# Moving half of an output projection's split weights and passes into the end of a gated scan, and the inverse root of two norms from logarithm and exponential

## The chip, the core and the metric

One core of one Trainium2 chip runs the whole program as one launch. The metric is the device time in microseconds of that launch. Five engines work side by side, each through its own list of instructions in order: TensorE (PE: matrix products, with its weight loads as PEld), VectorE (DVE), ScalarE (ACT), GpSimd (POOL) and SyncE (SP, which here only starts transfers). They wait for one another by semaphores.

## The reference, cut to what matters

The program is a deep stack; the change touches one stage of its second block and the norm ahead of two stages. For a stream of 256 tokens and a context of 256 tokens, with width 1024, that stage computes

```python
h = rms_norm(x, w) * (1 + scale) + shift            # y = x * rsqrt(mean(x*x) + 1e-6) * w
a = attention(h)                                    # 8 heads of 64: 512 columns
b = gated_scan(h)                                   # 4 heads of 128: 512 columns
x = x + gate * rms_norm(concat([a, b]) @ w_out, w2) # w_out: 1024 x 1024
```

Each head of the scan goes over all 512 tokens in two directions. A state decays by a factor per key column and token and takes in key times value; a query reads it. The kernel computes this as products between tokens with decays between them. A head's result is divided by its root mean square over its 128 columns and multiplied with a gate. The second block ends in a feed-forward part, and a second stage (local attention) follows with the same kind of norm ahead of it.

## The kernel before, in words

**Phases.** The program is a row of phases (`phase`, L200). Each has one instruction list per engine, and a barrier of all engines stands between two phases. Semaphores are the phase's own.

**Precision.** Products that need more than one pass are made from split numbers: `hi` is the value rounded to fp32r by a ScalarE copy, `lo` the rest, by a VectorE subtraction, and a product is hi x hi + hi x lo + lo x hi, three passes.

**The scan, `hgrn_phase` (L2782).** Four heads (`BH`), and for each eight units `u`: four tiles of 128 tokens in each of two directions. `sums` (L2945) makes the sums of the decays' logarithms in banks 0 to 2 of PSUM, `decay_tile` (L3106) is the ScalarE exponential that takes them, `products` (L3254) are the four VectorE products with keys and queries, `scores` (L2958) the TensorE products within sub-tiles (in bank 3, with the larger fragments in banks 4 and 5), `probs` (L3272) the VectorE mask and sum, `place` (L3209) the POOL product that puts them into the tile, `score_ends` (L3114) ScalarE's copies of the larger fragments, and `values` (L2983) the TensorE product with the values, added up in bank 7 (`O`). TensorE's list runs them with lags written out by hand: in unit u `sums(u)`, `scores(u-1)`, `values(u-3)`; between them, where a next head exists (`more`), the projection of that head (`slot`, L2914), a piece a unit. In the last head there is none.

**The end of a head (L3033 to L3048).** What one tile gives another is one set of six products per direction: `cross_operands` (L3282, VectorE), `cross_scores` (L2994, six products of fp32, which are twelve passes, into `X_PS`, bank 4 on), `keep_cross` (L3124, ScalarE, into `px`), `cross_values` (L3002, twelve passes into bank 7). Then `norm` on ScalarE (L3128: four squares with their sums, and a root) and VectorE (L3292), `turn_out` (L3009, four transposes) and `keep_output` (L3136), which writes the head's 128 columns into `y_T`. Chunks 0 to 3 of `y_T` are the attention's, and are there when the scan begins; chunks 4 to 7 are the four heads. SP loads the first four 512 KB blocks of `w_out` into `raw` (the space of `h_T`) at the end of its list (`load_ahead`, L2908).

**The projection, `out_both_phase` (L3338).** For each chunk n of 128 rows ScalarE makes `y_hi` and `w_hi` (L3389, L3391) and VectorE `y_lo` and `w_lo` (L3399, L3400). TensorE then has, for stream 0, twelve passes of 512 columns a chunk (two tiles of tokens, two halves of the columns, three parts) in banks 0 to 3; then the same for stream 1 in banks 4 to 7: 192 passes in all. After chunk 2 of stream 1 (`BEHIND`) it turns stream 0's scaled result (`turn_tensor`, L294). The last four blocks of `w_out` are asked for as their slots come free. The scalings behind are `post_scalar` (L328) and `post_vector` (L361).

**The pre-norm, `prenorm_phase` (L1994),** is called for the scan's stage (`first`) and for the second stage (with `bias`: there TensorE also makes a bias table, `Bias.products` L1971, which ScalarE and VectorE copy out, `Bias.keep` L1982). ScalarE squares five of eight tiles (L2027), VectorE three, and adds; TensorE sums over the partitions (L2058, L2060); ScalarE takes the root (L2031), VectorE the reciprocal (L2082), then h = x * r (L2088) and scale and shift on both engines (L2042, L2093). TensorE fills its idle time with products of zeros (`idle_products`, L305): 13, and 4 where there is a bias.

## Time and profile before

| | us |
|---|---|
| median of 3 runs | 2385.87 (2382.46 to 2386.08) |
| the profiled execution | 2385.46 |
| its span, first to last instruction | 2383.7 |
| PE busy | 2283.5 (96%) |
| DVE busy | 1442.6 (61%) |
| ACT busy | 1137.2 (48%) |
| POOL busy | 81.3 (3%) |
| mean granted clock of TensorE | 0.979 |

All times of one instruction are from the profiled execution and count from the start of its span. PE is busy 96% of the span as a whole, so what an edit is worth shows only in the stretch where it acts. The granted clock is a share of 2.4 GHz: 1.00 is 2.4 and 0.50 is 1.2 GHz. A matrix product of plain fp32 shows as two passes. Passes overlap: the time between two starts, not the length of one, is what a pass costs in a row of them. "L" and a number is a line of the kernel.

### The profile page before, as it was taken

The page shows a single profiled execution, that of the slowest core. Times are in us where ns is not written, and L with a number is a line of the kernel's source. Part 1 is how long each engine was busy: PE and PEld are TensorE (multiplying, and loading weights), DVE is VectorE, ACT ScalarE, POOL GpSimd, SP SyncE. Part 2 cuts the span into 40 slices and gives each one's busy share as a digit, 9 for nine tenths or more (in the row PEclk, how much of TensorE's full clock was granted, in tenths as well). Part 3 has the DMA queues.
Part 4 walks back from the last instruction along what each step waited for, and adds up shares of the span by engine and source line. Part 5 has one row for each costly group of instructions (what it writes and reads, how often), then busy time and mean ns, then how long its engine had stood idle before and what let it go on. Part 6 is the DMA issues. An engine that isn't in the chain of part 4 may idle for free. (4 is left out here: it accounts for less than half of the span.)

```text
span 2383.7 us, 37825 instructions
## 1 busy us (share of the span) xinstructions
PE 2283.5 (96%) x14434; PEld 1861.4 (78%) x14434; DVE 1442.6 (61%) x2358; ACT 1137.2 (48%) x1957; POOL 81.3 (3%) x117
## 2 busy tenths in 40 slices
PE   8999999999999999999999996999999989989998
...
GB/s 268 272 261 204 115 54 247 266 227 179 261 250 206 109 124 212 255 254 86 52 34 46 46 55 36 54 124 124 114 107 113 146 85 89 98 11 158 194 193 89
DMA packets 389939, 346.84 MB, mean 146 GB/s; under 512 B 24388, under 2 KB 353464, under 8 KB 389304
## 3 DMA queue, kind: packets, MB, share of 16 engines
...
HBM read 344.05 MB, written 1.05 MB: 145 GB/s over the span
## 5 line engine op out<-in xcount | busy, mean ns | idle before, releaser
L716 PE MATMUL ps<-x_hi_lo,gu_hi 128*128 128x512 f32 x1680 | 423.7, 394 | 3.3 <-DVE gu_sum L914 3.3
L716 PEld LDWEIGHTS ps<-x_hi_lo,gu_hi 128*128 128x128 f32 x1680 | 305.7, 188 | 82.4 <-issue 19.3
L914 DVE TENSOR_REDUCE gu_sum<-ps 128x256 f32<-128x512 f32 x220 | 150.1, 689 | 241.0 <-PE ps L718 240.8
L817 ACT ACTIVATE gu_hi<-w_gu 128x1024 fp32r<-128x1024 f32 x220 | 229.2, 1054 | 119.0 <-DMA w_gu<-in_ffn_w_up 45.1
L897 DVE TENSOR_TENSOR gu_lo<-w_gu,gu_hi 128x1024 fp32r<-128x1024 f32 x220 | 260.8, 1219 | 18.0 <-ACT gu_hi L817 17.7
L718 PEld LDWEIGHTS ps<-x_hi_lo,gu_lo 128*128 128x128 f32 x1680 | 228.8, 190 | 16.8
L718 PE MATMUL ps<-x_hi_lo,gu_lo 128*128 128x256 f32 x1680 | 233.8, 282 | 0.0
L745 PE MATMUL ps<-dn_hi,h_hi 128*128 128x512 f32 x440 | 173.3, 394 | 2.4 <-DVE h_lo L941 2.4
L745 PE MATMUL ps<-dn_lo,h_hi 128*128 128x512 f32 x440 | 172.5, 392 | 0.0
L745 PE MATMUL ps<-dn_hi,h_lo 128*128 128x512 f32 x440 | 171.3, 389 | 0.0
L833 ACT ACTIVATE silu<-gu_sum 128x256 f32<-128x256 f32 x88 | 36.7, 417 | 258.9 <-DVE gu_sum L914 258.3
L905 DVE TENSOR_TENSOR dn_lo<-w_dn,dn_hi 128x1024 fp32r<-128x1024 f32 x110 | 134.4, 1222 | 15.4 <-ACT dn_hi L821 10.7
L821 ACT ACTIVATE dn_hi<-w_dn 128x1024 fp32r<-128x1024 f32 x110 | 115.6, 1055 | 55.1 <-PE ps L745 55.1
L1077 PE MATMUL ps<-both_x_hi,gu_lo 128*128 128x512 f32 x320 | 124.5, 389 | 0.0
L1077 PE MATMUL ps<-both_x_lo,gu_hi 128*128 128x512 f32 x320 | 124.5, 389 | 0.0
L1077 PE MATMUL ps<-both_x_hi,gu_hi 128*128 128x512 f32 x320 | 124.5, 389 | 0.0
L1244 DVE SCALAR_TENSOR_TENSOR conv<-ps,par,conv 128x510 f32<-128x510 f32 x44 | 30.9, 744 | 129.4 <-ACT conv L1184 129.4
L745 PEld LDWEIGHTS ps<-dn_hi,h_hi 128*128 128x128 f32 x440 | 83.0, 189 | 17.9 <-issue 3.5
L745 PEld LDWEIGHTS ps<-dn_hi,h_lo 128*128 128x128 f32 x440 | 82.7, 188 | 18.1
L1184 ACT ACTIVATE conv<-ps,par 128x512 f32<-128x512 f32 x44 | 31.8, 775 | 131.7 <-PE ps L1077 121.0
L745 PEld LDWEIGHTS ps<-dn_lo,h_hi 128*128 128x128 f32 x440 | 83.1, 189 | 13.3
L308 PE MATMUL ps<-zero 128*128 128x512 f32 x122 | 66.3, 681 | 5.0 <-PEq L207 5.0
...
## 6 DMA issues: line engine op xcount, KB each, us to landing
...
```

What stands on the lines that cost most here:

```text
L308: pe.matmul(k.ps[:, bank, :], k.zero[:, :], k.zero[:, :].unsqueeze(1).broadcast_to([P, BANK // P, P]), start=True, stop=True, skip_group_c ...
L716: pe.matmul(gu(a), gu_hi[n][:, a, f, :], x_both[:, f, :, :], start=(f == 0), stop=False, skip_group_check=True)
L718: last = pe.matmul(gu(a)[:, 0, :], gu_lo[n][:, a, f, :], x_hi[:, f, :], start=False, stop=(f == FT - 1), skip_group_check=True)
L745: last = pe.matmul(k.ps[:, 2 * tt + c, :], h[n][:, tt * P:(tt + 1) * P], wt[n][:, c * BANK:(c + 1) * BANK], start=(first and p == 0), stop ...
L817: act.activation(gu_hi[n][:, a, :, :], wgu[n][:, a, :, :], ACT.Copy).then_inc(s["w_hi"], 1)
L821: act.activation(dn_hi[n][:, :], wdn[n][:, :], ACT.Copy).then_inc(s["w_hi"], 1)
L833: act.activation(sil[n][:, :], c[n][:, 0, :], ACT.Silu).then_inc(s["act_done"], 1)
L897: last = dve.tensor_tensor(gu_lo[n][:, a, :, :], wgu[n][:, a, :, :], gu_hi[n][:, a, :, :].bitcast(F32), ALU.subtract)
L905: dve.tensor_tensor(dn_lo[n][:, :], wdn[n][:, :], dn_hi[n][:, :].bitcast(F32), ALU.subtract).then_inc(s["dn_split"], 1)
L914: dve.reduce_sum(c[n][:, a, :], gu(a).rearrange("p h t -> p t h"), AX.X).then_inc(s["c_ready"], 1)
L1077: last = pe.matmul(gu(n, a), wt[n][:, a, f, :], x[:, f, :], start=(f == 0 and p == 0), stop=(f == FT - 1 and p == 2))
L1184: act.activation(cv[n][:, a, :, :].rearrange("p s t -> p (s t)"), gu(n, a), ACT.Identity, bias=conv.bias(t, a), scale=conv.tap(1, t, a)).t ...
```

## The change

Three things change.

1. In the last head of the scan the cross products of direction 0 come ahead of the last unit's scores. Their result goes to banks 0 and 1 instead of 4 and 5, and into memory of its own (`m.px`, the raw weights' space), and their operands are made in unit 5. For this the scores' bank and the next head's projection bank change places (3 and 6) in all heads.
2. Chunks 0 to 3 of the output projection are split within the last head: weights' and inputs' high parts by ScalarE in units 1 and 3 to 7 (into the space of `h_hi` and `w_hi`), low parts by VectorE around the norm. TensorE does stream 0's passes for these chunks there, 16 high ones and 32 low ones. Blocks 4 and 5 of `w_out` are asked for as their slots come free. The projection phase starts with stream 1's passes for chunks 0 to 3. The load of ScalarE's table for the root is drawn ahead of the last copies by an activation on one column.
3. In `prenorm_phase` the inverse root is Exp(-0.5 Ln(mean + eps)) on ScalarE instead of Sqrt and VectorE's reciprocal, an activation on one column at the phase's start names Ln first, and TensorE has 11 fillers instead of 13.

```diff
+act.activation(table[:, :], k.eps[:, 1:2], ACT.Ln)
-act.activation(std, k.ps[:, 0, 0:n], ACT.Sqrt, bias=k.eps[:, 1:2], scale=1.0 / D).then_inc(s["std_done"], 1)
+act.activation(std, k.ps[:, 0, 0:n], ACT.Ln, bias=k.eps[:, 1:2], scale=1.0 / D).then_inc(s["ln_done"], 1)
+act.wait_ge(s["ln_done"], 1)
+act.activation(r, std, ACT.Exp, scale=-0.5).then_inc(s["r_done"], 1)
...
-idle_products(pe, k, 7, 4 if bias else 13)
+idle_products(pe, k, 7, 4 if bias else 11)
...
-dve.wait_ge(s["std_done"], 1)
-dve.reciprocal(r, std).then_inc(s["r_done"], 1)
...
+    room = [a[:, :, :].rearrange("p f n -> p (f n)") for a in (m.h_hi, m.h_lo)]
+    m.out_w = [a[:, 0:OUT_AHEAD * D].rearrange("p (n d) -> p n d", d=D) for a in room]
+    room = [a[:, :, :, :].rearrange("p f r n -> p (f r n)") for a in (m.w_hi, m.w_lo)]
+    m.out_y = [a[:, 0:OUT_AHEAD * (S + CTX)].rearrange("p (n t) -> p n t", t=S + CTX) for a in room]
+    m.px = m.wh[:, :, :, :].rearrange("p r f n -> p (r f n)")[:, 0:6 * P].rearrange("p (n t) -> p n t", t=P)
+OUT_SLOTS = 4
+OUT_AHEAD = 4
...
+out_w_hi, out_w_lo, out_y_hi, out_y_lo = *m.out_w, *m.out_y
+root = sb("hgrn_root", [P, 1])
-    SC_PS = k.ps[:, 3, 0:NDIAG]
+    SC_PS = k.ps[:, 6, 0:NDIAG]
-    X_PS = flat[:, 4 * BANK:4 * BANK + 6 * P]
+    def X_PS(i, d):
+        at = 0 if i == LAST and d == 0 else 4 * BANK
+        return flat[:, at:at + 6 * P]
+    def PX(i, d):
+        return m.px if i == LAST and d == 0 else px[:, :, :]
...
-return k.ps[:, (4, 5, 6, 3, 7)[c] if h == 0 else 6, :]
+return k.ps[:, (4, 5, 6, 3, 7)[c] if h == 0 else 3, :]
...
-load_ahead(sp, s, ahead)
+for dst, src in ahead:
+    sp.dma_start(dst, src).then_inc(s["ahead_in"], 16)
+for n in range(2):
+    sp.wait_ge(s["out_lo"], n + 1)
+    sp.dma_start(raw[:, n, :], stream[OUT_SLOTS + n]).then_inc(s["ahead_in"], 16)
+sp.wait_ge(s["ahead_in"], 16 * (len(ahead) + 2))
...
-    if d == 0:
+    if i == LAST and d == 0:
+        pe.wait_ge(s["e_ready"], unit(i, NU - 1))
+    elif i == LAST or d == 0:
-        last = pe.matmul(X_PS[:, n * P:(n + 1) * P], key, qry, start=True, stop=True, skip_group_check=True)
+        last = pe.matmul(X_PS(i, d)[:, n * P:(n + 1) * P], key, qry, start=True, stop=True, skip_group_check=True)
+def out_high(tt):
+    pe.wait_ge(s["proj_used"], 5 * BH)
+    pe.wait_ge(s["x_used"] if tt == 0 else s["e_ready"], 2 * LAST + 1 if tt == 0 else unit(LAST, NU - 1))
+    for n in range(OUT_AHEAD):
+        pe.wait_ge(s["out_hi"], OUT_AHEAD + n + 1)
+        for c in range(2):
+            pe.matmul(k.ps[:, 2 * tt + c, :], out_y_hi[:, n, tt * P:(tt + 1) * P], out_w_hi[:, n, c * BANK:(c + 1) * BANK],
+                      start=(n == 0), stop=False, skip_group_check=True)
+def out_low(n):
+    pe.wait_ge(s["out_lo"], n + 1)
+    for tt in range(TT):
+        for c in range(2):
+            for y_part, w_part in ((out_y_hi, out_w_lo), (out_y_lo, out_w_hi)):
+                pe.matmul(k.ps[:, 2 * tt + c, :], y_part[:, n, tt * P:(tt + 1) * P], w_part[:, n, c * BANK:(c + 1) * BANK],
+                          start=False, stop=False, skip_group_check=True)
-        last = pe.matmul(k.ps[:, O, dst * P:(dst + 1) * P], px[:, n, :], values_of(i, src), start=False,
+        last = pe.matmul(k.ps[:, O, dst * P:(dst + 1) * P], PX(i, d)[:, n, :], values_of(i, src), start=False,
...
-    scores(i, NU - 1)
-    values(i, NU - 3)
-    cross_scores(i, 0)
-    if more:
+        scores(i, NU - 1)
+        values(i, NU - 3)
+        cross_scores(i, 0)
-    values(i, NU - 2)
-    cross_values(i, 0)
-    cross_scores(i, 1)
-    values(i, NU - 1)
-    if more:
+        values(i, NU - 2)
+        cross_values(i, 0)
+        cross_scores(i, 1)
+        values(i, NU - 1)
-    cross_values(i, 1)
+        cross_values(i, 1)
...
+cross_scores(LAST, 0)
+out_high(1)
+scores(LAST, NU - 1)
+values(LAST, NU - 3)
+cross_values(LAST, 0)
+values(LAST, NU - 2)
+out_high(0)
+cross_scores(LAST, 1)
+values(LAST, NU - 1)
+cross_values(LAST, 1)
+out_low(0)
+out_low(1)
 turn_out(LAST)
+out_low(2)
+out_low(3)
...
-act.activation(px[:, :, :].rearrange("p n t -> p (n t)"), X_PS, ACT.Copy).then_inc(s["x_used"], 1)
+act.activation(PX(i, d).rearrange("p n t -> p (n t)"), X_PS(i, d), ACT.Copy).then_inc(s["x_used"], 1)
...
+def out_weights(n):
+    act.wait_ge(s["ahead_in"], 16 * len(ahead))
+    act.activation(out_w_hi[:, n, :], raw[:, n, :], ACT.Copy).then_inc(s["out_hi"], 1)
+def out_inputs(n):
+    act.activation(out_y_hi[:, n, :], b.y_T[:, n, :], ACT.Copy).then_inc(s["out_hi"], 1)
...
+        if u in (1, 3, 4, 5) and not more:
+            out_weights((1, 3, 4, 5).index(u))
+        if u >= 6 and not more:
+            for n in (2 * (u - 6), 2 * (u - 6) + 1):
+                out_inputs(n)
-    score_ends(i, NU - 2)
-    score_ends(i, NU - 1)
-    keep_cross(i, 0)
-    if more:
+        score_ends(i, NU - 2)
+        score_ends(i, NU - 1)
+        keep_cross(i, 0)
-    keep_cross(i, 1)
+        keep_cross(i, 1)
...
+act.activation(root[:, :], k.zero[:, 0:1], ACT.Sqrt)
+act.wait_ge(s["w_lo"], 5 * BH)
+keep_cross(LAST, 0)
+score_ends(LAST, NU - 2)
+score_ends(LAST, NU - 1)
+keep_cross(LAST, 1)
...
-def cross_operands(i):
-    dve.wait_ge(s["side_done"], unit(i, NU - 1))
-    dve.wait_ge(s["tot_ready"], unit(i, NU - 1))
-    for d in range(2):
-        l0, l1 = order(d, 0)
-        c0, c1 = order(d, 1)
-        dve.tensor_scalar(kx[:, d, :], ke[:, d * TILES + c0, :], tot[:, d * TILES + c1:d * TILES + c1 + 1], None, ALU.mult)
-        dve.tensor_scalar(qx[:, d, :], qs[:, d * TILES + l1, :], tot[:, d * TILES + l0:d * TILES + l0 + 1], None,
-                          ALU.mult).then_inc(s["x_ready"], 1)
+def cross_operands(i, d, u):
+    dve.wait_ge(s["side_done"], unit(i, u))
+    dve.wait_ge(s["tot_ready"], unit(i, u))
+    l0, l1 = order(d, 0)
+    c0, c1 = order(d, 1)
+    dve.tensor_scalar(kx[:, d, :], ke[:, d * TILES + c0, :], tot[:, d * TILES + c1:d * TILES + c1 + 1], None, ALU.mult)
+    dve.tensor_scalar(qx[:, d, :], qs[:, d * TILES + l1, :], tot[:, d * TILES + l0:d * TILES + l0 + 1], None,
+                      ALU.mult).then_inc(s["x_ready"], 1)
+def out_parts(n):
+    dve.wait_ge(s["out_hi"], OUT_AHEAD + n + 1)
+    dve.tensor_tensor(out_y_lo[:, n, :], b.y_T[:, n, :], out_y_hi[:, n, :].bitcast(F32), ALU.subtract)
+    dve.tensor_tensor(out_w_lo[:, n, :], raw[:, n, :], out_w_hi[:, n, :].bitcast(F32), ALU.subtract).then_inc(s["out_lo"], 1)
...
-cross_operands(i)
+    if u == 5 and not more:
+        cross_operands(i, 0, TILES - 1)
+for d in range(2 if more else 1):
+    cross_operands(i, d if more else 1, NU - 1)
...
+out_parts(0)
+out_parts(1)
 norm(LAST)
+out_parts(2)
+out_parts(3)
...
-def out_both_phase(nc, k, b, l, stream, raw):
+def out_both_phase(nc, k, b, l, stream, raw, m):
...
-w_hi, w_lo = sb("both_w_hi", [P, FT, D]), sb("both_w_lo", [P, FT, D])
-y_hi, y_lo = sb("both_y_hi", [P, FT, S + CTX]), sb("both_y_lo", [P, FT, S + CTX])
+rest = FT - OUT_AHEAD
+late_w = [sb(f"both_w_{x}", [P, rest, D]) for x in ("hi", "lo")]
+late_y = [sb(f"both_y_{x}", [P, rest, S + CTX]) for x in ("hi", "lo")]
+HI, LO = range(2)
+def W(part, n):
+    return m.out_w[part][:, n, :] if n < OUT_AHEAD else late_w[part][:, n - OUT_AHEAD, :]
+def Y(part, n):
+    return m.out_y[part][:, n, :] if n < OUT_AHEAD else late_y[part][:, n - OUT_AHEAD, :]
...
-for n in range(SLOTS):
+for n in range(2):
+    sp.sem_inc(s[f"w{n}_in"], 32)
+for n in range(2, SLOTS):
-for n in range(SLOTS, FT):
-    sp.wait_ge(s["lo_made"], n - SLOTS + 1)
+for n in range(SLOTS + 2, FT):
-for st in range(2):
-    for n in range(FT):
-        if st == 0:
-            pe.wait_ge(s["lo_made"], n + 1)
-        elif n == BEHIND:
-            pe.wait_ge(s["z0_ready"], TT)
-            pe.wait_ge(s["z1_ready"], TT)
-            turn_tensor(pe, k, s, t[0].z, s["po_turned"], 0, 0)
-        for tt in range(TT):
-            at = st * S + tt * P
-            for c in range(2):
-                for p, (y, wt) in enumerate(((y_hi, w_hi), (y_hi, w_lo), (y_lo, w_hi))):
-                    last = pe.matmul(k.ps[:, 4 * st + 2 * tt + c, :], y[:, n, at:at + P], wt[:, n, c * BANK:(c + 1) * BANK],
-                                     start=(n == 0 and p == 0), stop=(n == FT - 1 and p == 2), skip_group_check=True)
-            if n == FT - 1:
-                last.then_inc(s["tile_done"], 1)
+def chunk(st, n):
+    for tt in range(TT):
+        at = st * S + tt * P
+        for c in range(2):
+            for p, (y, wt) in enumerate(((HI, HI), (HI, LO), (LO, HI))):
+                last = pe.matmul(k.ps[:, 4 * st + 2 * tt + c, :], Y(y, n)[:, at:at + P], W(wt, n)[:, c * BANK:(c + 1) * BANK],
+                                 start=(st == 1 and n == 0 and p == 0), stop=(n == FT - 1 and p == 2), skip_group_check=True)
+        if n == FT - 1:
+            last.then_inc(s["tile_done"], 1)
+for n in range(OUT_AHEAD):
+    chunk(1, n)
+for n in range(OUT_AHEAD, FT):
+    pe.wait_ge(s["lo_made"], n - OUT_AHEAD + 1)
+    chunk(0, n)
+for n in range(OUT_AHEAD, FT):
+    if n == OUT_AHEAD + BEHIND:
+        pe.wait_ge(s["z0_ready"], TT)
+        pe.wait_ge(s["z1_ready"], TT)
+        turn_tensor(pe, k, s, t[0].z, s["po_turned"], 0, 0)
+    chunk(1, n)
-for n in range(FT):
-    act.activation(y_hi[:, n, :], b.y_T[:, n, :], ACT.Copy)
+for n in range(OUT_AHEAD, FT):
+    act.activation(Y(HI, n), b.y_T[:, n, :], ACT.Copy)
-    act.activation(w_hi[:, n, :], raw[:, n % SLOTS, :], ACT.Copy).then_inc(s["hi_made"], 1)
+    act.activation(W(HI, n), raw[:, n % SLOTS, :], ACT.Copy).then_inc(s["hi_made"], 1)
-for n in range(FT):
-    dve.wait_ge(s["hi_made"], n + 1)
-    dve.tensor_tensor(y_lo[:, n, :], b.y_T[:, n, :], y_hi[:, n, :].bitcast(F32), ALU.subtract)
-    dve.tensor_tensor(w_lo[:, n, :], raw[:, n % SLOTS, :], w_hi[:, n, :].bitcast(F32), ALU.subtract).then_inc(s["lo_made"], 1)
+for n in range(OUT_AHEAD, FT):
+    dve.wait_ge(s["hi_made"], n - OUT_AHEAD + 1)
+    dve.tensor_tensor(Y(LO, n), b.y_T[:, n, :], Y(HI, n).bitcast(F32), ALU.subtract)
+    dve.tensor_tensor(W(LO, n), raw[:, n % SLOTS, :], W(HI, n).bitcast(F32), ALU.subtract).then_inc(s["lo_made"], 1)
```

## Rows read from the trace of the kernel before

**Rows 1.** Windows: us, busy PE, PEld, DVE, ACT, POOL, granted clock, DMA, GB/s

```profile
1440.00:1456.00 16.00, 11.06 (x254) 8.72 (x252) 15.49 (x26) 7.30 (x19) 8.68 (x9) 1.00 0.01 3
...
1456.00:1466.00 10.00, 6.68 (x76) 5.97 (x77) 3.50 (x11) 2.26 (x9) 1.46 (x3) 0.54 0.00 1
...
1472.00:1481.00 9.00, 1.14 (x5) 0.74 (x5) 3.21 (x8) 6.11 (x13) 0.00 (x0) 0.60 0.00 1
...
1484.00:1512.00 28.00, 28.00 (x124) 23.12 (x124) 11.60 (x16) 9.32 (x15) 0.00 (x0) 1.00 0.17 55
```

**Rows 2.** Timeline, scan's end: start, us, engine, line, operation, [idle <-releaser]

```profile
1457.28 0.76 PE L2974 MATMUL ps<-hgrn_qd,hgrn_kd 128*32 128x32 f32 x40 [2.12 <-DVE hgrn_pm L3276]
...
1460.96 1.19 PE L2999 MATMUL ps<-hgrn_qs,hgrn_ke 128*128 128x128 f32 x4 [1.57 <-ACT hgrn_p L3121]
...
1463.89 0.81 ACT L3126 ACTIVATE hgrn_px<-ps 128x768 f32<-128x768 f32 x1 [3.08 <-PE ps L2999]
...
1464.76 2.64 PE L3005 MATMUL ps<-hgrn_vg,hgrn_px 128*128 128x128 f32 x12 [0.47 <-ACT hgrn_px L3126]
...
1469.63 1.61 PE L3005 MATMUL ps<-hgrn_vg,hgrn_px 128*128 128x128 f32 x12 [0.68 <-ACT hgrn_px L3126]
...
1472.43 1.28 ACT L3134 ACT_TABLE_LOAD   x1
...
1476.61 0.60 ACT L3138 ACTIVATE y_T<-ps 128x512 f32<-128x512 f32 x1 [2.58 <-PE ps L3012]
```

**Rows 3.** Output projection, timeline of PE

```profile
1480.98 0.79 PE L3379 MATMUL ps<-both_w_hi,both_y_hi 128*128 128x512 f32 x1 [4.41 <-DVE both_w_lo L3400]
...
1512.47 1.91 PE L300 MATMUL ps<-ident,ln_z_b 128*128 128x128 f32 x16
...
1527.60 0.39 PE L3379 MATMUL ps<-both_w_hi,both_y_lo 128*128 128x512 f32 x1
```

**Rows 4.** Its splits by tile (ns min/median/max, starts us); one in time

```profile
L3391 ACT ACTIVATE both_w_hi<-h_T x8: 1039/1052/1062, 1478.0 to 1490.7; 128x1024 fp32r<-128x1024 f32 x8
...
L3400 DVE TENSOR_TENSOR both_w_lo<-h_T,both_w_hi x8: 1214/1216/1218, 1479.7 to 1492.5; 128x1024 fp32r<-128x1024 f32 x8
...
1486.72 1.06 ACT L3391 ACTIVATE both_w_hi<-h_T 128x1024 fp32r<-128x1024 f32 x1 [1.01 <-DMA h_T<-in_even_w_out]
```

**Rows 5.** Timeline of ACT and DVE in the last head

```profile
1448.68 0.61 ACT L3121 ACTIVATE hgrn_p<-ps 32x32 f32<-32x32 f32 x3 [2.01 <-POOL hgrn_p L3215]
...
1449.27 1.13 ACT L3112 ACTIVATE hgrn_e<-ps 128x1152 f32<-128x1152 f32 x1
...
1450.68 1.08 DVE L3266 TENSOR_TENSOR hgrn_kd<-hgrn_e,hgrn_k 128x896 f32<-128x896 f32 x1
...
1457.62 0.28 DVE L3288 TENSOR_SCALAR hgrn_kx<-hgrn_ke,hgrn_tot 128x128 f32<-128x128 f32 x1
```

**Rows 6.** By line, both pre-norms: ns min/median/max, first and last start us

```profile
L2031 ACT ACTIVATE squares<-ps,eps x2: 687/687/687, 1116.1 to 1932.8; 128x512 f32<-128x512 f32 x2
...
L2082 DVE RECIPROCAL squares<-squares x2: 3352/3352/3353, 1116.8 to 1933.5; 128x512 f32<-128x512 f32 x2
```

**Rows 7.** Timeline: first pre-norm; ACT after a logarithm in the scan

```profile
1110.01 2.71 ACT L2027 ACTIVATE squares<-x_T 128x512 f32<-128x512 f32 x5 [0.47 <-PEq L207]
...
1113.42 1.42 DVE L2075 TENSOR_TENSOR squares<-squares 128x512 f32<-128x512 f32 x2
...
1125.70 2.55 ACT L2042 ACTIVATE h_T<-h_T,mod 128x256 f32<-128x256 f32 x5
...
1282.58 1.34 ACT L3087 ACTIVATE hgrn_abs<-hgrn_abs,eps 128x512 f32<-128x512 f32 x2
...
1283.93 1.28 ACT L3112 ACT_TABLE_LOAD   x1
```

**Rows 8.** Timeline, second pre-norm: ACT and PE

```profile
1944.58 4.50 ACT L2034 ACTIVATE na_bias<-ps 128x80 f32<-128x80 f32 x30 [3.90 <-DVE h_T L2088]
...
1945.63 10.55 PE L1979 MATMUL ps<-rpb_T,bias_pick 64*128 64x96 f32 x48 [2.50 <-ACT na_bias L2034]
```

12 lines of the change are left out of this document (6 added, 6 removed).

## The prediction, made blind

> **What bounds the kernel now.** I read the windows first, then the timeline of the scan's end, then that of the output projection behind it. In units 4 to 6 of the last head VectorE is busy 15.49 of 16 us and TensorE 11.06; the granted clock is 1.00, so 2.4 GHz [rows 1]. Then the picture turns: from 1456 to 1466 the clock is 0.54, nearly all at 1.2 GHz, and from 1472 to 1481 TensorE works 1.14 us of 9. The end of the scan is a chain that goes from engine to engine with one thing running at a time [rows 2]: TensorE waits 2.12 us for VectorE's mask, does the last scores, waits 1.57 us for ScalarE's fragment copies, does 12 cross passes of 128 columns from 1460.96 to 1463.86; ScalarE copies them in 0.81; 12 value passes; the same again for the other direction; then norm, with a table load of 1.28, and the last output copy, which ends at 1477.21. The projection has 192 passes of 512 columns. Its first waits 4.41 us for VectorE's first split, and from there to the end, 1527.99, TensorE never stops [rows 3]. At full clock it starts 124 passes in 28 us [rows 1], 0.226 us each; at the low clock I take twice that, 0.45. So what the change is worth is read from TensorE alone: from 1477.21 to 1527.99, 50.8 us, and from the end of the chain before it.
>
> **Projection.** Splits of chunks 0 to 3 and 48 of the 192 passes go into the scan. 144 remain: 144 x 0.226 = 32.5, the 16 transposes that stand between them 1.9 less overlap (1.7), drain 0.4, together 34.7. The first 48 of these need only what the scan left, so the 3.77 us from 1477.21 to 1480.98 shrinks to the 0.3 us by which a phase begins behind the one before it (ScalarE's first weight copy began at 1478.0 behind an input copy of 0.6 [rows 4]; the size of that copy is the one of 1476.61). 35.0 against 50.8: **-15.8**. Of this 10.9 are the 48 passes, 3.5 the start, 1.4 the low clock after the idle start. What covers the remaining splits: a chunk costs ScalarE 0.6 + 1.05 and VectorE 1.22 + 0.7 (an estimate: half the columns) [rows 4], so four are done after about 9 us, before the 10.9 us of the first 48 passes are over. Without that cover each chunk would stand out by 1.9. Chunks 6 and 7 are fetched at the phase's start and are wanted 16 us later: nothing. The turn of stream 0 keeps its 36 passes of distance from that stream's last; behind it are 12 passes (2.7) instead of 60, and VectorE's addition for stream 0 (about 4.5 after the turn begins) ends as the last pass does (1.7 + 2.7 + 0.4 = 4.8): nothing, with 0.3 us to spare.
>
> **The last head's loop.** ScalarE gets four weight copies of 1.05 and four input copies of 0.6. Three of the weight copies fall where it waits 0.7 us or more for TensorE; VectorE does not see them. The fourth stands in unit 5 between the fragment copies, ended 1449.29, and the exponential of 1449.27 [rows 5], which had no idle time ahead of it. It moves the exponential to 1450.24, its end to 1451.37, and VectorE's product from 1450.68 to 1451.41: +0.73. In the same place VectorE has two new products (0.28 and about 0.3 to 0.5, moved there from the end, where they stood at 1457.62), which are done by 1451.3: no more than the wait. Unit 6 repeats it with two input copies, 1.1 us: exponential ends 1454.98 instead of 1453.95, and VectorE's last products are 0.87 late in all. **+0.9** ahead of the end. Bounds: 0 and the whole 6.6 us of copies; I take 0.9 because each piece can be set against the idle time of its own place.
>
> **The scan's end, new order.** Before, TensorE had run dry at 1455.2 (1457.28 less 2.12); with the loop's 0.7 it is free at about 1455.8 and goes at once into the cross scores (12 passes, 1.6 at full clock, as the row of 1469.63 shows for 12 passes of the same size [rows 2]; 2.9 at half): 1457.4. Eight of the projection's high passes for the second tile, 1.8, held by the last input copy: 1459.0. Last scores, about 0.9 at full clock (1.3 at half): 1459.9. Mask and sum, POOL and the fragment copies took 2.3 from there to 1460.96; with 0.7 more for a POOL that shares its time with VectorE's splits they end about 1462.9. ScalarE meanwhile loads the root's table (1.28, no longer on the chain), keeps the first cross block (0.81) at 1460.4. TensorE: its value passes 1462.0, eight high passes for the first tile 1463.9, cross scores 1465.4; ScalarE 1466.3; value passes 1467.9. From the last value pass (1471.24) to the output copy (1476.61) it was 5.4 us [rows 2]; without the load 4.1, of which the turn is the last 1.1, so VectorE's result stands 3.0 after 1467.9, at 1470.9. Under these lie 16 low passes (3.6), 1467.9 to 1471.5; then the turn, 1472.7. VectorE's two last split pairs (1.9 each) end 1472.7 and 1474.5, the last eight passes 1476.4. Against 1477.2: **-0.8**, the +0.9 within it. What is late next is VectorE's last split, not the norm. SP waits at the phase's end for two more weight blocks asked for at 1462.6 and 1464.5; the projection's own first such request, asked for near 1480.95, held up a ScalarE copy until 1486.72 [rows 4], under 6 us, so some 4 us are over.
>
> **Pre-norms.** The reciprocal is 3.35 us in each, and what replaces it is an exponential of at most the 0.69 of the root row [rows 6]. But in the scan, ScalarE's exponential behind a logarithm is preceded by a load of 1.28 [rows 7], so one stands between Ln and Exp here too, and one before the phase's first activation. In the first pre-norm: the squares, from 1110.01, begin 1.4 later (load 1.28, activation 0.2 less overlap). The fourth of the five squares (0.54 apart) then ends at 1113.6, and VectorE's additions move from 1113.42 by only 0.26, since they had room [rows 7]. Ln 1116.3 (1116.06 plus that) to 1117.0, load to 1118.3, Exp to 1119.0, first h at 1119.03 instead of 1120.16: **-1.1**, which the last scaling (from 1125.70, 2.55 long) carries to the phase's end; the 11 fillers left end earlier still. Bounds: -2.4 without the load in between, and +0.3 if TensorE's wait for the first square, grown from 1.6 to 3.0 us, costs the clock. The next phase's first root needs a new load: 0.4 late on VectorE in a stage where TensorE has 10 us of work per tile: nothing. In the second pre-norm TensorE's bias products shift 1.4, and with them the sum, at low clock; so Ln starts 1.4 later, r is ready at the old time, and the stage ends as before by ScalarE's copies, which waited for VectorE's h, and the 48 products that waited 2.50 us for those copies [rows 8]: **0**, bounds -1.3 and +1.4.
> Here the Trainium skill speaks twice. "ScalarE: Activation LUTs", section "Table sets: the hidden batching unit", says Ln then Exp is one load, as one set holds both; the trace disagrees with its 1.28 between them. By it the sum would be 2.6 less. The same page, "What ACT_TABLE_LOAD costs", gives a switch a drain of about 1.38 us beside the load, which speaks against this change; in the row of 1283.93 the load starts 0.01 behind the logarithms, and the trace shows no drain.
>
> **Sum.** -15.8 - 0.8 - 1.1 = -17.7. The profiled execution took 2385.46 (span 2383.7); the median of the three runs, 2385.87, is 0.4 above: 2368.2, said as 2368. The banks that change places (scores and projection) move no instruction: nothing, bound 0.5 either way. 0.2% is 4.8 us, about what a measurement tells from no change.
>
> **Rivals.**
> *A, the clock falls within the new end.* For: it fell at about this place before, after half-empty unit periods, and the loop's two delays make one more gap. Against: from 1455.8 TensorE has work in a row. Price: 12 cross passes +1.3, eight high +1.8, scores +0.4, 12 value passes +1.0: 4.5, so 2372.5; with the pre-norm's +1.4 2374. Chance 0.20.
> *B, Ln and Exp share a load.* -1.3 in each pre-norm: 2365.6. Against: the load between them in the scan [rows 7], though these phases are other code. Chance 0.07.
> *C, the copies stretch every unit,* since VectorE has only 0.5 us in 16 to catch up: 6.6 instead of 0.9, 2373.9. Against: TensorE released the other exponentials, not ScalarE. Chance 0.08.
> *D, a load costs double,* 1.28 more each, an idle piece of its own size beside it. The drain that the Trainium skill ("ScalarE: Activation LUTs") gives would be such a piece. In both pre-norms r comes 2.6 later: 2373.4. Chance 0.02.
> *E, the moved work is paid in full:* 1.2 GHz through the whole end. 48 passes at 0.45 are 21.6 us, cross and value passes keep their old 2.6 to 2.9; the phase would end some 14 to 15 later than reckoned, the projection begin slowly (1.4): 2384. No change. Chance 0.03.
> *F, slower.* The place is E's, and the low clock goes on into the projection, 0.226 a pass: from 30 slow passes on, 13 us, it is over 2390.6; through the 48 of stream 1, 2384 + 9.5 = 2393. Against: at 1480.98, from idle, the clock was back within 3 us, and it is 1.00 from 1484 on [rows 1]. Chance 0.03.
> The forecast, 2366 to 2370.5 by the small bounds, has 0.57.
>
> **How the numbers follow.** Range 2364.5 to 2374.5: B at one end, A, C and D at the other; E and F are left out. Faster 0.94 (all but E and F), same 0.03, slower 0.03.
>
> **What would show it.** Right: first projection pass within 0.4 us of the scan's last instruction and at 0.39 us; 144 passes; from there to the last 34.7. Exponential in unit 5 about 1 us later behind a copy of 1.05, the table load beside cross passes, the last low passes waiting for VectorE. Two loads in each pre-norm, h 1.1 us earlier in the first, nothing in the second. Wrong: a clock near 0.5 between cross scores and norm (A), no load before the exponential (B), idle VectorE in units 2 to 5 (C), a scan that ends over 1 us later than before, measured from its last head's first unit.

## The result, and the profile after

| | before | after |
|---|---|---|
| median of the first runs | 2385.87 (5 runs, 2382.46 to 2389.65) | 2363.83 (5 runs, 2359.77 to 2367.07) |
| mean of all runs of this study | 2384.3 (68 runs) | 2364.3 (11 runs) |
| profiled execution | 2385.46 | 2363.83 |
| its span | 2383.7 | 2362.1 |
| PE busy | 2283.5 | 2274.1 |
| mean granted clock | 0.979 | 0.984 |

The ratio is 0.9908, 95% interval 0.9889 to 0.9928; six later runs of the same kernel, beside eleven of before, gave 0.9912 (0.9893 to 0.9931). The change is faster, by 0.9%. My forecast of 2368.0 had the direction. Its range, 2364.5 to 2374.5, missed the median by 0.7 us.

Since a busy share of 96% says nothing on where 20 us went, I cut the span into stages, each by one instruction that both kernels have. The kernel before has them at 1110.04 (first square of the first pre-norm on VectorE), 1128.54 (first product of the next phase), 1458.24 (last cross operand of the last head), 1477.49 (the projection's first ScalarE copy), 1527.60 (its last pass), 1923.91 (VectorE's first square of the second pre-norm), 1978.62 (the 97th product of the phase behind it).

| us | before | after | difference | my sum |
|---|---|---|---|---|
| S0: to the first pre-norm, untouched | 1110.04 | 1107.95 | -2.1 | 0 |
| S1: first pre-norm | 18.50 | 18.49 | 0.0 | -1.1 |
| S2: scan, to the last cross operand | 329.70 | 329.53 | -0.2 | |
| S3: scan's end | 19.24 | 18.62 | -0.6 | S2 and S3: -0.8 |
| S4: projection | 50.12 | 34.35 | -15.8 | -15.8 |
| S5: to the second pre-norm, untouched | 396.31 | 395.88 | -0.4 | 0 |
| S6: second pre-norm and the next phase's start | 54.71 | 51.59 | -3.1 | 0 |
| S7: the rest, untouched | 405.07 | 405.65 | +0.6 | 0 |

**The scan's end** answers to [rows 1, 2]. The timeline of TensorE (start, length, engine, line, operation, and in brackets the idle time ahead of it and who ended it):

```profile
1454.58 2.09 PE L3033 MATMUL ps<-hgrn_h_hi,hgrn_w_hi 128*128 128x512 f32 x8
...
1458.17 1.60 PE L3047 MATMUL ps<-hgrn_vg,hgrn_w 128*128 128x128 f32 x12 [0.21 <-ACT hgrn_w L3180]
...
1459.76 2.09 PE L3033 MATMUL ps<-hgrn_h_hi,hgrn_w_hi 128*128 128x512 f32 x8
...
1464.08 1.60 PE L3047 MATMUL ps<-hgrn_vg,hgrn_px 128*128 128x128 f32 x12 [0.68 <-ACT hgrn_px L3180]
...
1469.19 0.60 PE L3054 MATMUL ps<-ident,hgrn_z 128*128 128x128 f32 x4
...
1470.36 0.50 PE L3041 MATMUL ps<-hgrn_h_lo,hgrn_w_hi 128*128 128x512 f32 x1 [0.57 <-DVE hgrn_h_lo L3365]
...
1474.61 0.47 PE L3461 MATMUL ps<-hgrn_h_hi,hgrn_w_hi 128*128 128x512 f32 x1 [0.30 <-PEq L207]
...
1508.93 0.39 PE L3461 MATMUL ps<-both_w_hi,both_y_lo 128*128 128x512 f32 x1
```

Where TensorE waited 2.12 and 1.57 us before, it now waits 0.21, and the twelve value passes take 1.60, not 2.64. The last low passes wait for VectorE's split, as forecast, but 0.57 us only. The projection's first pass follows the scan's last within 0.4, and takes 0.47 instead of 0.79. The windows of the same stretch (length; busy PE, PEld, DVE, ACT, POOL; granted clock; DMA share; GB/s):

```profile
1454.00:1464.00 10.00, 9.20 (x108) 7.75 (x106) 7.21 (x13) 6.00 (x15) 2.18 (x3) 1.00 0.22 62
1464.00:1474.30 10.30, 9.65 (x48) 7.68 (x48) 4.78 (x9) 2.07 (x11) 0.00 (x0) 1.00 0.12 44
1474.30:1500.00 25.70, 25.40 (x113) 21.05 (x113) 9.53 (x13) 9.62 (x16) 0.00 (x0) 1.00 0.11 42
```

The clock, 0.54 and 0.60 at the two places before, is 1.00 throughout. ScalarE's load of the root's table, the first cross copy behind it and the root (between them stand the fragment copies, the other cross copy and the squares):

```profile
1455.80 1.28 ACT L3260 ACT_TABLE_LOAD   x1
...
1457.31 0.81 ACT L3180 ACTIVATE hgrn_w<-ps 128x768 f32<-128x768 f32 x1
...
1466.90 0.30 ACT L3188 ACTIVATE hgrn_std<-hgrn_ss,eps 128x4 f32<-128x4 f32 x1
```

The root at 1466.90 has no load right ahead of it; that of 1472.43 [rows 2] is now at 1455.80, beside the high passes.

**The first pre-norm** of after, TensorE and then ScalarE:

```profile
1109.98 4.52 PE L2062 MATMUL ps<-squares,ones 128*128 128x512 f32 x6 [2.98 <-ACT squares L2029]
1114.34 1.02 PE L2064 MATMUL ps<-squares,ones 128*128 128x512 f32 x2
```

```profile
1107.91 1.28 ACT L2027 ACT_TABLE_LOAD   x1 [0.46 <-PEq L207]
...
1115.40 0.69 ACT L2033 ACTIVATE squares<-ps,eps 128x512 f32<-128x512 f32 x1 [3.39 <-PE ps L2064]
1116.10 1.28 ACT L2035 ACT_TABLE_LOAD   x1
1117.40 0.63 ACT L2035 ACTIVATE squares<-squares 128x512 f32<-128x512 f32 x1
```

Both loads are there, one between logarithm and exponential [rows 7 had it in the scan]; it begins 0.01 us behind the logarithm, with no drain. But the six passes of the ones-products take 4.52 us, where the old pre-norm's take 2.84: TensorE had been idle for 2.98, and part of them ran at 1.2 GHz (the granted clock over these 4.52 us is 0.62).

**The second pre-norm.** First TensorE before, then after:

```profile
1927.01 4.89 PE L2058 MATMUL ps<-squares,ones 128*128 128x512 f32 x6
...
1939.51 3.62 PE L1979 MATMUL ps<-rpb_T,bias_pick 64*128 64x96 f32 x16
...
1956.12 6.55 PE L308 MATMUL ps<-zero 128*128 128x512 f32 x8
1965.72 5.38 PE L2549 MATMUL ps<-odd_w_hi,odd_h_hi 128*128 128x256 f32 x32 [3.05 <-ACT odd_h_hi L2700]
```

```profile
1909.35 4.20 PE L2062 MATMUL ps<-squares,ones 128*128 128x512 f32 x6
...
1922.46 13.93 PE L1979 MATMUL ps<-rpb_T,bias_pick 64*128 64x96 f32 x64
1936.32 5.22 PE L308 MATMUL ps<-zero 128*128 128x512 f32 x8
1944.59 4.30 PE L2551 MATMUL ps<-odd_w_hi,odd_h_hi 128*128 128x256 f32 x32 [3.05 <-ACT odd_h_hi L2702]
```

The 2.50 us of waiting between 16 and 48 bias products [rows 8] are gone, they run as 64 in one piece, and both the fillers (6.55 to 5.22) and the next phase's first 32 products (5.38 to 4.30) run faster: the clock is back sooner. Here lies the main error of my sum.

### The profile page after: what moved, and what is told of

Same layout as the page of the kernel before. It is cut to its first block and busy times, and to the rows that moved or that the text cites. A ratio compares the mean times of both kernels' runs of the same rounds, so it can differ in the third digit from the quotient of the medians.

```text
span 2362.1 us, 37833 instructions
## 1 busy us (share of the span) xinstructions
PE 2274.1 (96%) x14430; PEld 1855.6 (79%) x14430; DVE 1436.8 (61%) x2356; ACT 1142.3 (48%) x1966; POOL 80.3 (3%) x117
## 5 line engine op out<-in xcount | busy, mean ns | idle before, releaser
L716 PEld LDWEIGHTS ps<-x_hi_lo,gu_hi 128*128 128x128 f32 x1680 | 305.6, 188 | 82.9 <-issue 19.4
L897 DVE TENSOR_TENSOR gu_lo<-w_gu,gu_hi 128x1024 fp32r<-128x1024 f32 x220 | 260.9, 1220 | 19.6 <-ACT gu_hi L817 19.4
L821 ACT ACTIVATE dn_hi<-w_dn 128x1024 fp32r<-128x1024 f32 x110 | 115.5, 1055 | 54.6 <-PE ps L745 54.6
L745 PEld LDWEIGHTS ps<-dn_hi,h_hi 128*128 128x128 f32 x440 | 83.0, 189 | 17.8 <-issue 3.4
L745 PEld LDWEIGHTS ps<-dn_hi,h_lo 128*128 128x128 f32 x440 | 82.6, 188 | 18.2
L1077 PEld LDWEIGHTS ps<-both_x_hi,gu_lo 128*128 128x128 f32 x320 | 60.1, 188 | 12.6
```

The lines of the kernel that those rows point to most:

```text
L716: pe.matmul(gu(a), gu_hi[n][:, a, f, :], x_both[:, f, :, :], start=(f == 0), stop=False, skip_group_check=True)
L745: last = pe.matmul(k.ps[:, 2 * tt + c, :], h[n][:, tt * P:(tt + 1) * P], wt[n][:, c * BANK:(c + 1) * BANK], start=(first and p == 0), stop ...
L821: act.activation(dn_hi[n][:, :], wdn[n][:, :], ACT.Copy).then_inc(s["w_hi"], 1)
L897: last = dve.tensor_tensor(gu_lo[n][:, a, :, :], wgu[n][:, a, :, :], gu_hi[n][:, a, :, :].bitcast(F32), ALU.subtract)
L1077: last = pe.matmul(gu(n, a), wt[n][:, a, f, :], x[:, f, :], start=(f == 0 and p == 0), stop=(f == FT - 1 and p == 2))
```

## The experiments

What was in doubt: whether the extra gain belongs to the second pre-norm's new root (theory S in the expectations) or to the granted clock, which falls at other places from one execution to the next (theory C); why the first pre-norm gained nothing; and whether the projection's 15.8 came as I reckoned. One traced execution of each kernel by stages, us, and all its runs:

| | S0 | S1 | S2 | S3 | S4 | S5 | S6 | S7 | runs: mean | ratio to before, 95% |
|---|---|---|---|---|---|---|---|---|---|---|
| before | 1110.0 | 18.5 | 329.7 | 19.2 | 50.1 | 396.3 | 54.7 | 405.1 | 68: 2384.3 | |
| after | 1108.0 | 18.5 | 329.5 | 18.6 | 34.3 | 395.9 | 51.6 | 405.6 | 5: 2363.5 | 0.9908 (0.9889, 0.9928) |
| a1_norms | 1112.9 | 18.3 | 329.7 | 19.2 | 50.1 | 396.0 | 51.8 | 405.5 | 10: 2380.4 | 0.9981 (0.9970, 0.9992) |
| a2_scan | 1112.7 | 18.5 | 327.8 | 18.6 | 34.3 | 396.0 | 53.9 | 406.3 | 5: 2366.7 | 0.9919 (0.9906, 0.9933) |
| a3_norm2 | 1114.3 | 18.5 | 329.6 | 19.2 | 50.1 | 396.3 | 51.5 | 405.4 | 11: 2382.9 | 0.9986 (0.9975, 0.9997) |
| a4_norm1 | 1114.2 | 18.2 | 329.6 | 19.2 | 50.1 | 396.0 | 55.1 | 405.1 | 11: 2385.1 | 1.0004 (0.9993, 1.0016) |
| b1_no_preload | 1110.0 | 17.1 | 326.5 | 18.6 | 34.3 | 395.9 | 52.0 | 405.0 | 4: 2362.2 | 0.9903 (0.9887, 0.9920) |
| b2_hold | 1107.1 | 21.6 | 326.5 | 18.6 | 34.3 | 396.0 | 52.2 | 405.2 | 4: 2364.6 | 0.9914 (0.9897, 0.9930) |
| b3_norm2_late | 1109.0 | 18.5 | 326.6 | 18.2 | 50.8 | 394.8 | 53.8 | 405.4 | 10: 2384.6 | 1.0003 (0.9992, 1.0014) |
| b4_root_late | 1113.3 | 19.8 | 326.6 | 19.4 | 34.3 | 395.9 | 51.7 | 405.6 | 4: 2368.2 | 0.9927 (0.9902, 0.9951) |
| c1_no_fill | 1107.7 | 18.5 | 326.3 | 25.8 | 34.3 | 395.8 | 52.7 | 406.2 | 10: 2376.1 | 0.9975 (0.9961, 0.9988) |
| c2_split_first | 1107.4 | 17.1 | 327.7 | 17.8 | 34.3 | 394.1 | 51.1 | 405.1 | 4: 2359.7 | 0.9912 (0.9896, 0.9929) |
| c3_split_and_low | 1112.7 | 17.1 | 326.2 | 17.7 | 34.3 | 394.1 | 51.3 | 405.2 | 4: 2358.9 | 0.9902 (0.9885, 0.9918) |
| c5_hold3 | 1112.4 | 17.3 | 326.3 | 18.6 | 34.3 | 395.9 | 52.0 | 405.2 | 4: 2364.4 | 0.9928 (0.9911, 0.9944) |
| d1_changed_again | 1115.4 | 17.3 | 329.2 | 18.6 | 34.3 | 395.8 | 52.0 | 405.1 | 6: 2364.9 | 0.9912 (0.9893, 0.9931) |
| d2_best_again | 1111.9 | 17.1 | 327.8 | 17.8 | 34.4 | 395.9 | 51.9 | 405.0 | 6: 2360.9 | 0.9897 (0.9878, 0.9915) |

S0, where all these kernels have the same code, spreads over 8.3 us, S2 over 3.5. Where the code is the same, S1, S3, S4 and S6 mostly repeat to some tenths; the exceptions are b3, whose S3 is 1.0 shorter and whose S4 0.7 longer than in the four other traces of that code, S1 where the new root has its early fetch (17.3 to 19.8), and S6 by up to 1.6. So verdicts come from stages, and a ratio is only set beside them.

**The change's halves.**

```diff
 # a1_norms: the kernel before, with the changed prenorm_phase
 # a2_scan: the changed kernel, with prenorm_phase of before
 # a3_norm2, a4_norm1: as a1_norms, in one of the two calls only
-act.activation(std, ps, ACT.Sqrt, ...)
+act.activation(std, ps, ACT.Ln if bias else ACT.Sqrt, ...)     # a3; a4: if not bias
```

> The kernel before with the change's two pre-norms alone (logarithm and exponential, 11 fillers), scan and projection as before. Theory S (the second pre-norm gains by the change itself; the first gains nothing, since TensorE's longer wait ahead of its first ones-product costs the clock): first pre-norm 0, second -2.4, time 2.4 below the kernel before, and the trace shows the logarithm of the second pre-norm 12.3 us behind the phase's start or sooner. Theory C (the 4.4 us by which the change beat my sum are the granted clock of stages that it doesn't touch, and of the second pre-norm, which falls differently from run to run): no difference of over 0.5 us on average, with single runs 2 to 4 apart. My prediction's own terms: -1.1.

> The changed kernel with the pre-norms of before (root and reciprocal, 13 fillers): the scan's end and the projection alone. My terms for it: -0.8 and -15.8, so 2369.2 against 2385.9. Theory S says the same, 16.6 below before and 2.4 above the changed kernel. Theory C: 16.6 to 21 below before, equal to the changed kernel within 1, since what the changed kernel has more comes from the clock of other stages.

> The kernel before with logarithm and exponential in the second pre-norm alone (4 fillers as before). Theory S: -2.4. My prediction's term: 0. Theory C: 0 on average, and in the trace the second pre-norm's end is -2.4 or 0 with the same work in it.

> The kernel before with logarithm and exponential (and 11 fillers) in the first pre-norm alone. My prediction's term: -1.1. What the trace of the changed kernel shows: 0, as the six ones-products then ran at 1.2 GHz (4.52 us instead of 2.84), because TensorE idled 2.98 us ahead of them. If that is due to the change, the same 4.5 us stand in this trace; if it was the chance of one run, 2.84 and -1.1.

S6 is 51.8 and 51.5 where the second pre-norm is changed (a1, a3) and 53.9 and 55.1 where it isn't (a2, a4): the gain is the change's own. Over all traces S6 averages 51.8 with the change in its plain form (12) and 54.6 without it (3): -2.8. Theory C's "0 on average" falls. The intervals of a1's and a3's ratios, both below 1, say the same. a2 gives S3 and S4 as the changed kernel has them, and 0.9919 is -19.3 us with an interval of -22.4 to -16.0 that holds my -16.6 (its mean is 17.7 below that of the runs beside it). In a4 the low clock of the first pre-norm stands again behind the same wait (against 2.84 us for six with the old root):

```profile
1116.24 4.25 PE L2064 MATMUL ps<-squares,ones 128*128 128x512 f32 x6 [2.98 <-ACT squares L2030]
```

**The first pre-norm's missing 1.1.**

```diff
 # b1_no_preload
-act.activation(table[:, :], k.eps[:, 1:2], ACT.Ln)
 # b2_hold: n = 8; c5_hold3: n = 3, ahead of the first ones-product
+if not bias:
+    idle_products(pe, k, 7, n)
```

> The changed kernel without the activation on a dummy that fetches the logarithm's table at each pre-norm's start. A load stands ahead of the wait of the instruction that needs it, so the table would be fetched in ScalarE's 3.4 us of idle time ahead of the logarithm. Squares begin 1.4 us sooner, TensorE waits 1.6 us for the first instead of 3.0. If that wait is what costs the clock in the first pre-norm (theory S), its six ones-products take 2.84 again and the stretch from this pre-norm's start to the next phase's first product is 17.1 instead of 18.5. Rival: the clock falls there in any case, 18.2. Second pre-norm: the gain of 3.1 stays if it comes from the sooner r, and goes if it comes from the shift of the squares.

> The changed kernel with 8 idle products of 512 columns (1.9 us) at the start of the first pre-norm, under the table load and the first square. If TensorE's 2.98 us without work are what takes the clock down (theory S), the six ones-products take 2.84 us instead of 4.52 and the stretch from this pre-norm's start to the next phase is 17.4 (the -1.1 of my sum). Rival: the clock falls by what lies before this phase, and the stretch stays 18.5.

> The changed kernel with 3 idle products at the first pre-norm's start. One costs 0.86 us (11 took 9.6), which I had mis-sized in the run with 8 of them, whose 6.8 us held the ones-products up; 3 take 2.6 and are done before the first square at 2.98. If TensorE's idle 2.98 us are what takes the clock down: six ones-products 2.8 instead of 4.5, stretch to the next phase 17.4 instead of 18.5. Rival: 18.5 with the low clock, since an idle product doesn't hold it.

TensorE of b1, then of c5:

```profile
1110.65 2.84 PE L2061 MATMUL ps<-squares,ones 128*128 128x512 f32 x6 [1.61 <-ACT squares L2028]
```

```profile
1112.44 2.81 PE L308 MATMUL ps<-zero 128*128 128x512 f32 x6 [0.95 <-PEq L207]
1115.09 2.74 PE L2064 MATMUL ps<-squares,ones 128*128 128x512 f32 x6
```

Both came out as theory S has it, 17.1 and 17.3. Without the early fetch the load falls into ScalarE's idle time, between its last square and the logarithm:

```profile
1112.70 1.28 ACT L2032 ACT_TABLE_LOAD   x1
1116.01 0.69 ACT L2032 ACTIVATE squares<-ps,eps 128x512 f32<-128x512 f32 x1 [2.03 <-PE ps L2063]
```

TensorE then waits 1.61, and the clock stays. With the wait filled it stays too. b2 is a miss of mine, S1 21.6 for an expected 17.4: an idle product of this form is two passes and costs 0.86, so eight held the ones-products until 1114.06; yet those six then took 2.74. Of six traces with the early fetch and nothing in TensorE's 2.98 us, five have the low clock (18.2 to 19.8) and one, d1, has not:

```profile
1117.46 2.84 PE L2062 MATMUL ps<-squares,ones 128*128 128x512 f32 x6 [2.98 <-ACT squares L2029]
```

It took 17.3, my forecast to a tenth. None of the six traces without that idle time has it low, nor have the four with the old root. So the long gap is what brings the low clock within reach; why d1 escaped it, no trace tells.

**Why the second pre-norm gains.**

```diff
 # b3_norm2_late: a3_norm2, and behind the wait for r on VectorE
+dve.reciprocal(total[:, 0:168], std[:, 0:168])     # nobody reads it
```

> The kernel before with logarithm and exponential in the second pre-norm alone, and behind the exponential a reciprocal of 168 columns on VectorE that nobody reads, which costs 1.1 us: r is ready at the time of before. Theory R (the second pre-norm gains because r comes 1.1 us sooner, which spares TensorE its wait for ScalarE's copies and brings the clock back sooner): the stretch from its start to the next phase is 41 us again and the next phase's first products take 5.4 instead of 4.3, so 3 us above the kernel with the change in the second pre-norm alone. Theory Q (what counts is that the squares and the first products stand 0.4 to 1.4 later, against which the clock is counted): 39 to 40 and 4.3.

```profile
1940.91 10.55 PE L1979 MATMUL ps<-rpb_T,bias_pick 64*128 64x96 f32 x48 [2.15 <-ACT na_bias L2040]
1951.40 5.33 PE L308 MATMUL ps<-zero 128*128 128x512 f32 x8
1959.78 4.30 PE L2558 MATMUL ps<-odd_w_hi,odd_h_hi 128*128 128x256 f32 x32 [3.05 <-ACT odd_h_hi L2709]
```

The delay brought back the wait (2.15) and 2.3 of the 3.2 us, and the ratio is 1.0003. It delayed more than I meant, though. VectorE's useless reciprocal took 1.20, and in this trace the six ones-products took 5.49 us, where a3's took 4.35; so the first h came 2.3 later than in a3, and 1.35 later than in the kernel before. Cut into pieces, us, from VectorE's first square of this phase (h is the first h = x * r on VectorE, the copy ScalarE's first `odd_h_hi` of the next phase):

| | to the first h | to the first filler | the fillers | to the copy | to the 97th product | S6 |
|---|---|---|---|---|---|---|
| before | 12.99 | 19.21 | 6.55 | 2.29 | 13.66 | 54.71 |
| a4_norm1, old root here | 13.38 | 19.39 | 6.46 | 2.29 | 13.62 | 55.14 |
| a2_scan, old root here | 13.63 | 19.21 | 4.95 | 2.29 | 13.86 | 53.94 |
| the 12 with the new root, mean | 12.24 | 19.23 | 5.37 | 2.29 | 12.68 | 51.81 |
| b3_norm2_late | 14.34 | 19.22 | 5.33 | 2.29 | 12.57 | 53.75 |

From the first h to the fillers it is 19.2 to 19.4 us in all 16 traces, whether TensorE waits 2.1 to 2.7 us among its bias products or not. So the wait was slack, and its loss is no gain by itself: what r gains, the phase's end gains, one to one. That is b3's 2.3 against a3, and it is 1.1 of the change's 2.8. Another 0.6 is the fillers, which run at a higher clock on average, with one old trace (a2) faster than any new one. This much of theory R holds.

The last 1.0 is the next phase's start, from its first copy to its 97th product: 13.6 to 13.9 us in all three traces with the old pre-norm and in c1, and 12.6 in all others. It is the clock's (the first 32 products take 5.3 to 5.6 in those four and 4.3 in the rest), but neither theory explains it. R would have it long in b3, where r is late and the wait is back, and it is not. Q would have it long in b1, whose ones-products begin as early behind VectorE's first square as a2's (3.56), and it is 12.6 there too, with S6 at 52.0. Its cause stays open.

One thing more stands in all these traces. The fillers end this phase 3.9 to 5.5 us behind its last bias copy (in the changed kernel 36.73 against 32.54 behind VectorE's first square). Whether fewer of them would shorten it, or cost as much in the next phase's clock, no run has tried.

**The scan's end and the projection.**

```diff
 # b4_root_late
-act.activation(root[:, :], k.zero[:, 0:1], ACT.Sqrt)
 # c1_no_fill
-out_high(1) ... out_high(0) ... out_low(0); out_low(1)
 turn_out(LAST)
+out_high(1); out_high(0); out_low(0); out_low(1)
```

> The changed kernel without the early root on ScalarE, so that the root's table is fetched in front of the last head's root, on the chain from the last value pass to the norm. If that chain and VectorE's splits of chunks 2 and 3 behind it set the scan's end, as my prediction has it, the end is 1.3 us later (the size of the load) in the stretch from the first pre-norm's end to the projection's first copy: 349.4. Rival: the load hides under the 16 low passes that lie beneath the chain, 348.1 as in the changed kernel.

> The changed kernel with the 32 early passes of the projection issued behind the last head's turn of the output instead of within the scan's end; splits, copies and the new order of the cross products stay. Theory P (my prediction's terms: the gain is that work is laid under the chain, and the low clock goes with it): the stretch from the last head's last cross operand to the projection's first copy is 18.6 in the changed kernel; here the chain ends about as before or up to 2 sooner and 7.3 us (32 at 0.226) or 14.4 (at 1.2 GHz) stand behind it, 24 to 31, and the granted clock falls within it. Rival: the reordered cross products and the root's early table alone shorten the chain by 3 or more, under 23.

b4: the load of 1.28 stands on the chain again, and S3 is 19.4, +0.8, between the 1.3 that I expected and the rival's 0. The chain sets the end, but 0.5 us of the load was covered:

```profile
1470.09 1.28 ACT L3188 ACT_TABLE_LOAD   x1
1471.38 0.30 ACT L3188 ACTIVATE hgrn_std<-hgrn_ss,eps 128x4 f32<-128x4 f32 x1
```

c1: S3 is 25.8, +7.2, and TensorE waits 2.94 where it had work. That this is just what 32 passes cost (32 x 0.226 = 7.2) is in part luck: the turn begins 0.8 sooner and a wait of 0.57 is gone, and some of the passes run slower.

```profile
1464.94 1.11 PE L3054 MATMUL ps<-ident,hgrn_z 128*128 128x128 f32 x4 [2.94 <-DVE hgrn_z L3371]
1465.70 5.12 PE L3033 MATMUL ps<-hgrn_h_hi,hgrn_w_hi 128*128 128x512 f32 x16
```

The turn begins 12.4 us behind the last cross operand here, and 13.2 in the changed kernel, where 16 low passes stand ahead of it. In the kernel before it is 17.2:

```profile
1475.45 1.12 PE L3012 MATMUL ps<-ident,hgrn_z 128*128 128x128 f32 x4 [4.21 <-DVE hgrn_z L3298]
```

So the reordered cross products and the early load do shorten the chain by themselves, by 4.8 us: 1.28 is the load, and 3.5 is that the cross values of direction 1 begin 7.9 behind the last cross operand instead of 11.4. Against b3, which has the old code here and more of the high clock (turn at 16.2), it is 3.8. The rival had this right, and theory P's "as before or up to 2 sooner" holds against the changed kernel alone. The rival's "under 23" is too low, since all 48 passes stand behind the turn here, not 32. They are 10.8 us at full clock, and the first 16 took 5.12 where 15 starts at 0.226 and a last pass of 0.39 are 3.8. What the change gains at this place is both: the chain to the last output copy ends 14.5 us behind the operand instead of 19.0, and the time is filled with the projection's 48 passes, which run on for 3.9 us behind that copy. That is why S3 itself moves by 0.6 alone. The ten runs of c1 average 12 above the changed kernel, more than its trace shows: this is the lowest of them, 2369.2, and I take the others to have had more of the low clock, which isn't shown, since none of them was traced.

**Two repairs.**

```diff
 # c2_split_first: b1_no_preload and, VectorE
 out_parts(1)
+out_parts(2)
 norm(LAST)
-out_parts(2)
 # c3_split_and_low: c2, and TensorE's out_low(2) ahead of turn_out(LAST)
 # d2_best_again: c3, unaltered; d1_changed_again: the changed kernel, unaltered
```

> The kernel without the tables' early fetch, and in the scan's end VectorE splits the third chunk in its 5.04 us of idle time ahead of the norm's reciprocal instead of behind the norm. My prediction has VectorE's last split as what is late at the scan's end; the trace of the changed kernel shows TensorE only 0.57 behind the output it wants. Theory P: the last low passes start at once behind the turn, 0.6 us sooner end (18.0 instead of 18.6 for the stretch from the last cross operand to the projection's first copy). Rival: nothing is gained, 18.6, since the turn itself holds them.

> As the one before, and TensorE takes the third chunk's 8 low passes (1.8 us) ahead of the turn instead of behind it, where it waited 0.23 us for VectorE's result and then had the turn's 0.6 alone. The last chunk's split then has 1.8 us more of cover: stretch 17.6 to 18.0, and the time 2361, with pre-norms at 17.1 and 52 (second pre-norm and the next phase's first products).

> The changed kernel, unaltered. By stages, traces so far give it -0.2 (first pre-norm), -0.7 (scan's end), -15.8 (projection) and -3.1 (second pre-norm with the next phase's first products): 19.8 below the kernel before, whose 57 runs average 2384.2, so 2364.4. Theory C holds that what its first five runs had beyond that (21.9) was the clock's chance in stages that the change leaves alone: then this is 19 to 21. Rival: the change has a further effect of some 2 us that no stage's trace shows, and it is 22 to 24.

> The changed kernel without the early fetch of the logarithm's table, third chunk split ahead of the norm and its low passes ahead of the turn. Against the changed kernel: 1.4 in the first pre-norm, 0.9 in the scan's end, and 1.8 behind the projection if its trace's shorter low clock there is the rule: 2.3 to 4.1 below the run beside it.

VectorE's timeline of c2: the third split stands in idle time, and 3.31 of it are still left.

```profile
1458.92 1.21 DVE L3364 TENSOR_TENSOR hgrn_h_lo<-h_T,hgrn_h_hi 128x1024 fp32r<-128x1024 f32 x1
1463.44 0.18 DVE L3368 RECIPROCAL hgrn_r<-hgrn_std 128x4 f32<-128x4 f32 x1 [3.31 <-ACT hgrn_std L3187]
```

S3 falls to 17.8 (-0.9; -0.6 was expected), and taking the low passes ahead of the turn adds nothing (17.7): once TensorE has no gap, their order is worth nothing. The 1.8 us that both gained in S5 are not in d2's trace of the same kernel, so they are the clock's. d1 came at 20.0 below before by its mean (2384.97 less 2364.93), inside theory C's 19 to 21, and outside the rival's 22 to 24; but the interval of its ratio, -25.5 to -16.5 us, holds both, so this doesn't decide between them. d2, on the same chip, is 4.0 below d1 in the mean and its ratio 0.9897 against 0.9912; the intervals overlap, so that c3 beats the changed kernel rests on the stages, 1.4 and 0.9.

## Why the prediction was right or wrong

**Projection, -15.8: right.** Measured -15.77. First pass to end 34.7 us, as summed; the first pass comes 0.4 behind the scan's last and at 0.47.

**Scan's end, -0.8: right, its pieces partly.** S2 and S3 give -0.8. The 0.6 of it in S3 is against a trace whose old code ran there at 0.54; b3 has 18.2 for the same old code, so a term of this size can't be told from the clock at this place. With S4 beside it, it is 69.4 to 53.0 against before and 69.0 to 53.0 against b3. The loop's +0.9 was too much: the exponential of unit 5 came 0.9 later, as said, and VectorE's products behind it 0.65, but in unit 6 POOL's placing took less, ScalarE's fragment copies came sooner, and 0.4 was left. What that saved was lost at the end: I had the last eight passes wait for the fourth chunk's split, but it was the third's that held TensorE, and 16 passes came behind it. A split of VectorE's was late next, as named, and c2 shows what it cost: 0.9.

**First pre-norm, -1.1: a mechanism right, its condition not.** I had the bound, "+0.3 if TensorE's wait for the first square, grown from 1.6 to 3.0 us, costs the clock", and took the other end. It does so in five of six traces. Their mean with the sixth is 18.4, so this term is -0.1.

**Second pre-norm, 0: the step that failed.** I wrote "Ln starts 1.4 later, r is ready at the old time, and the stage ends as before", with bounds of -1.3 and +1.4. The logarithm starts 9.67 us behind ScalarE's first instruction, instead of 9.30: 0.4 later, since the ones-products, pushed back by 1.1, took 0.7 less. r is ready 1.1 sooner, and the phase's end follows it; the wait of 2.50 that the bias products lose was slack. The fillers behind run faster. Measured -2.8 on average, outside my bounds: 1.1 from the sooner r, 0.6 from the fillers and 1.0 from the next phase's first products, the last with its cause open. I had let "at low clock" stand as a constant, where the clock was the thing that moved, and I had put nothing down for what comes behind the bias products.

**The base.** Three runs gave 2385.87; 68 average 2384.3. S0 alone differs by up to 8.3 us between executions. An example, the windows of the same untouched stretch, before and then after:

```profile
285.00:295.00 10.00, 10.00 (x47) 6.09 (x46) 2.65 (x7) 6.20 (x21) 0.43 (x1) 0.66 0.90 353
```

```profile
285.00:295.00 10.00, 9.43 (x65) 6.99 (x66) 4.58 (x15) 7.39 (x26) 0.53 (x1) 1.00 0.83 317
```

The clock fell there in one execution (0.66). From 287 to 293 the kernel before falls some 3 us behind the other, instruction by instruction on VectorE, and smaller differences elsewhere leave the 2.1 us of S0 in the result's table. They belong to no edit.

**The sum again.** -15.8 - 0.8 - 0.1 - 2.8 = -19.5, against -20.0 between the means of all runs. Of the 4.4 us between my 2368.2 and 2363.8, 1.8 are the terms, 1.6 the base (2385.9 for 2384.3), 0.5 the difference that the stages don't explain, 0.5 what five runs had below eleven.

**Rivals.** A, the clock within the new end: in none of the ten traces with the new order and its fill is S3 above before's, but for b4's 0.2 with its load. B, one load for both: no, two loads everywhere. C, stretched units: no, 0.4. D, double loads: no, 1.28 each. E and F: no, the clock is 1.00 there; even in c1, without the fill, it is 0.87 over the 13 us behind the turn, and its S4 is 34.3. The banks that change places: nothing, as said, S2 is 326.6 in b3 with the old ones and 326.5 in b1 with the new. The range failed in its lower end: it held B and no scatter of the base, and the one bound of a gain in the second pre-norm was too small. With that term alone put right the sum gives 2365.4 (2368.2 less 2.8). That the median then lies 0.7 outside the range, and not further in or out, is chance: the five runs go from 2359.8 to 2367.1.
